# A decoder layer on one core: modulation products in groups of four, and a vector's sums inside its last step

## The chip, the core and the metric

The kernel runs on one core of a Trainium2 chip. The metric is the device time of one execution in microseconds; less is better. The engines of the core are named as in the profile: PE (the matrix engine; PEld are its weight loads), DVE (the vector engine), ACT (the scalar engine), POOL and SP. SP only issues DMA transfers here.

## The reference

One layer of a hybrid decoder for a prompt of 256 tokens and 8 sample tokens, all in float32, with a model width D of 2048 and a feed-forward width of 5632. Eleven modulation vectors (nine of the layer, two of the final norm) come from the condition c; the feed-forward blocks and the mixer use them as shift, scale and gate:

```python
mod = jax.nn.silu(c) @ p['w_ada'] + p['b_ada']
sh1, sc1, g1, sh2, sc2, g2, sh3, sc3, g3 = jnp.split(mod, N_MOD, axis=-1)
h = modulate(rmsnorm(x, p['g_ffn1']), sh1, sc1)
x = x + 0.5 * g1[:, None, :] * swiglu(h, p['w_up1'], p['w_down1'])
h = modulate(rmsnorm(x, p['g_mix']), sh2, sc2)
o, new_state = hybrid_mixer(h, lru_h0, lru_buf0, ssm_h0, ssd_buf0, p)
x = x + g2[:, None, :] * o
h = modulate(rmsnorm(x, p['g_ffn2']), sh3, sc3)
x = x + 0.5 * g3[:, None, :] * swiglu(h, p['w_up2'], p['w_down2'])
```

The matrix of one modulation vector is 2048 x 2048, 16 MB; all eleven together are 176 MB of the some 524 MB that the kernel reads.

## The kernel before, in words

The columns of the activations are the 264 tokens (COLS). Each weight is split into a high and a low part, and each product is made of three matmuls in the fp32r form: high by high, high by low, low by high (lines 1393 to 1395, in `piece`). The weights stream through the core in **steps**. A step of a feed-forward "up" or of the mixer is 8 **pieces** of 4 k-tiles by 256 weight columns, each piece 24 matmuls; a "down" step has 8 pieces of 3 or 2 k-tiles, 22 in all. For each step SP issues four weight loads (j = 0 to 3, two pieces each) into `raw` (line 489), each of which waits until DVE is done with the pieces that lay in the slot before (`lo_done`). ACT writes the high part of a piece into `w_hi` (line 608), DVE the low part into `w_lo` (line 872), and PE uses both. `w_hi` and `w_lo` have four slots, so ACT begins on piece m + 4 when PE has used piece m.

A list `plan` written out by hand sets the order: up and down steps of the first block in two chunks, then the mixer ("xbc", "dt", "lru", "z", "out"), then the second block. Each segment of the plan is a run of steps that an engine walks through either as code laid out straight or as a loop (`turns`). Segments of 4 steps per turn also carry a **modulation vector**: 16 products (`ada_product`, line 1357), four in each step, one ahead of every second piece. Two vectors are made at the start, ahead of the first step. The other nine are made inside steps: first block, chunk 0, vectors 2 and 3 in 8 up steps and vector 4 in 4 down steps; chunk 1, vectors 5 and 6 in 8 up steps and 7 in 4 down steps; second block, vector 8 in 4 up steps of chunk 0, vectors 9 and 10 in 8 up steps of chunk 1. The remaining up steps (3 or 7 of 11 in a chunk) and down steps have no products. Vectors 5 and 6, and 9 and 10, are two turns of a loop on PE; vectors 2 and 3 are laid out straight.

A product multiplies one k-tile of silu(c), `cT`, a stationary operand of 32 columns, by a slab of 128 x 2048 of the vector's matrix, in four matmuls that lie side by side in the array by `tile_position`, each with 512 columns; all sixteen add into bank b4. The slab is a load of 1 MB that SP issues (`ada_load`, line 468) into one of two slots of `ada` behind each weight load, when product a - 2 has been used. The two vectors at the start use two more slots, `ada_more`, which lie where the activations of the feed-forward blocks are later (`act_hi`).

When a vector's last step is over, its **sums** are placed: ACT copies b4 to `ada_sum` (line 621, `ada_copy`), PE transposes four blocks (line 1337, `ada_turn`), and DVE adds the bias and writes `mods` (line 894, `mod_place`). The first product of the next vector waits for that (`mod_ready`), since it writes b4. Before the change these three are the last thing that each engine does in the turn. Gates are taken from `mods` by `make_gate` into a tile of their own, and `add_branch` (line 945) adds the branch to x with it. PE starts a feed-forward block when DVE has written `h_lo` of the norm (line 923) and the first pieces.

Of the kernel before, what the change touches and what calls it, by code (L numbers as in the profile page):

```python
# [21 lines left out]
F32 = mybir.dt.float32  # L22
F32R = mybir.dt.float32r
ALU = mybir.AluOpType
# [3 lines left out]
P = 128  # L28
# [120 lines left out]
def build(nc, ins, outs):  # L149
    with ExitStack() as ctx:  # L150
# [16 lines left out]
        gate = sb("gate", [P, KD, 9])  # L167
# [21 lines left out]
        def layout(entries):  # L189
# [16 lines left out]
        _, _, ada_more, rowbuf, xrows = layout([  # L206
            ("ada_s", [P, 2, D], F32), ("ada_sum_s", [P, 512], F32), ("ada_more", [P, 2, D], F32),
            ("rowbuf", [P, ROW_TILES, P], F32), ("xrows", [P, 2, D], F32)])
        _, _, yrows, ysrow = layout([
            ("ada_e", [P, 2, D], F32), ("ada_sum_e", [P, 512], F32),  # L210
            ("yrows", [P, 2, D], F32), ("ysrow", [P, P], F32)])
# [37 lines left out]
        ada_landed = [sem(f"ada_landed{j}") for j in range(2)]  # L249
        first_landed = [sem(f"first_landed{j}") for j in range(4)]  # L250
# [205 lines left out]
        def _(sp):  # L456

            def ada_load(a, vec, k):

                if not isinstance(a, int) or a >= 2:  # L460
                    sp.wait_ge(ada_used, a - 1)
# [6 lines left out]
                sp.dma_start(ada[:, k % 2, :], src).then_inc(ada_landed[k % 2], 16)  # L468

            row_copies(sp, True, c_rows)  # L470
            for a in range(2 * KD):
                if a >= 4:
                    sp.wait_ge(ada_used, a - 3)
                dst = (ada, ada_more)[(a // 2) % 2][:, a % 2, :]
                sp.dma_start(dst, w_ada[:, a % KD, bass.ds(a // KD * D, D)]).then_inc(first_landed[a % 4], 16)
# [34 lines left out]
        def _(pool):  # L510
# [8 lines left out]
            pool.memset(outcol[:, OUT_ROWS:], 0.0)  # L519
# [3 lines left out]
            pool.wait_ge(piece_used, 8 * S_XBC)  # L523
            pool.memset(spt[:, :], 0.0)  # L524
# [73 lines left out]
        def _(act):  # L598
# [265 lines left out]
        def _(dve):  # L864
# [37 lines left out]
            def make_gate(vec, factor):  # L902
                dve.wait_ge(mod_ready, vec + 1)
                ch.link(TS(gate[:, :, :], mods[:, vec, :, :], factor, None, ALU.mult))
# [34 lines left out]
            def add_branch(s, par, before, n0, squares):  # L939
# [3 lines left out]
                for h in range(2):  # L943
                    xt = x[:, bass.ds(n0 + h, 1), 0:NT]
                    STT(xt, ps[:, h:h + 1, 0:NT], gate[:, bass.ds(n0 + h, 1), 0:1].rearrange("p a b -> p (a b)"),  # L945
                        xt, ALU.mult, ALU.add)
                xs = x[:, bass.ds(n0, 2), :]
                TT(part[:, :, NT:COLS], ps[:, :, NT:COLS], gate[:, bass.ds(n0, 2), 1:9],
# [126 lines left out]
            def dve_tasks(kind, t, j, s, o_, e_):  # L1075
# [147 lines left out]
                if kind == "z" and u == 7:  # L1223
# [22 lines left out]
                    make_gate(G2, 1.0)  # L1246
                    ch.link(dve.memset(sumsq[:, :, :], 0.0))
                if kind == "out" and j in (1, 3):
                    par = j // 2
                    add_branch(8 * (S_OUT + t) + (8 if par else 4), par, (e_, o_)[par], 2 * (2 * t + par), True)  # L1250
# [7 lines left out]
            for n, seg in enumerate(plan):  # L1258
# [14 lines left out]
                for i, last in turns(dve, seg, peel_first=n == 0, peel_last=differs(n), chain=ch, links=links):  # L1273
                    for k in range(per):
                        s, e_, o_, par = at_step(seg, i, k)
                        follows = nxt if last and k == per - 1 else PIECE_KIND[kind]
                        for j in range(4):
                            pieces_ahead(s, j, PIECE_KIND[kind], follows)
                            if kind == "up" and j == 3:
# [13 lines left out]
                            if kind == "down" and j == 3:  # L1293
                                n0 = i * (2 * per) + 2 * (what[2] + k)
                                add_branch(s * 8 + 8, par, (e_, o_)[par], n0, squares)
# [364 lines left out]
```

## Time and profile before

| What | Value |
|---|---|
| Median of 3 runs | 2333.21 us (2332.66 to 2335.88) |
| The profiled execution: its span | 2337.2 us |
| PE matmuls busy | 2185.2 us, 93% |
| DVE busy | 1200.1 us, 51% |
| ACT busy | 839.7 us, 36% |
| Read from memory | 524.37 MB, 227 GB/s over the span |
| Mean granted clock of PE | 0.967 |

The page gives no time of the profiled execution besides its span, which runs from the first to the last instruction; it is 0.17% above the median of the runs. The busy time of PE is a sum over pipelined instructions and says little by itself; the timeline shows where matmuls don't follow each other. The granted clock is 1.00 at the upper of its two levels and 0.50 at the lower one.

### The profile page before, as it was taken

Reading aid. Unit: us, or ns where it says so; the run is one execution under the profiler, and the core shown is the slowest. Engines: PE = TensorE matmul, PEld = TensorE weight load, DVE = VectorE, ACT = ScalarE, POOL = GpSimd, SP = SyncE. Lnnn points to the kernel's source line nnn. Section 1 sums busy time; section 2 is a strip of 40 time slices with the busy share of each in tenths; the row PEclk is TensorE's granted clock in tenths of the full one; section 3 lists DMA queues with packets and bytes.
Section 4 is the critical chain, followed back from the end, with each engine's and each line's share of the span. In section 5 each row is a group of like instructions: output and inputs, shape, how many; then the busy total and the mean of one; then the engine's idle time right before and its main releaser. Section 6 shows DMA issues by size and latency. Waiting matters only on the chain.

```text
span 2337.2 us, 40988 instructions
## 1 busy us (share of the span) xinstructions
PE 2185.2 (93%) x17053; PEld 1974.6 (84%) x17053; DVE 1200.1 (51%) x1602; ACT 839.7 (36%) x1020; POOL 128.9 (6%) x146
## 2 busy tenths in 40 slices
PE   4589999999999999989978889899999999999997
PEld 1178889889878898989967889789999988789996
DVE  1254345345434444576779876634445544344555
ACT  0043233334323332345544443433333433233333
POOL 0000000000000000001556200000000000000000
PEclk8799999999999999999998999999999999999998
DMA  8978895786878858746444445685545589895452
GB/s 339 365 252 297 281 305 187 256 294 225 299 262 294 280 184 298 259 138 202 158 136 135 143 158 197 220 308 194 179 153 176 187 292 302 261 307 191 149 184 86
DMA packets 380728, 533.59 MB, mean 228 GB/s; under 512 B 11815, under 2 KB 356783, under 8 KB 357807
## 3 DMA queue, kind: packets, MB, share of 16 engines
q1 hardware_dynamic: 358288, 519.28, 66.2%
q10 hardware_dynamic: 22303, 12.33, 1.8%
q8 instruction: 105, 1.72, 0.3%
q14 instruction: 32, 0.26, 0.0%
HBM read 524.37 MB, written 7.19 MB: 227 GB/s over the span
## 4 chain that ended last, share of the span: by engine, by line
PE 84%; DVE 9%; DMA 3%; ACT 2%; issue 1%; ACTq 1%; DVEq 0%; SPq 0%
PE main L1393 26%; PE main L1394 25%; PE main L1395 25%; PE b L1357 7%; DVE w_lo L872 2%; DMA ada_more<-in_w_ada 1%; DMA heads_row<-in_ssd_D 1%; DVE rec L1194 1%; ACTq L445 0%; PE b L1337 0%; ACT w_hi L608 0%; DVE cfull L1001 0%; DMA rowbuf<-in_b_ada 0%; DMA raw<-in_w_in 0%; DVE xdec L1038 0%
## 5 line engine op out<-in xcount | busy, mean ns | idle before, releaser
L872 DVE TENSOR_TENSOR w_lo<-raw,w_hi 128x1024 fp32r<-128x1024 f32 (+2 forms) x720 | 796.0, 1113 | 948.2 <-ACT w_hi L608 942.2
L1393 PE MATMUL main<-h_hi,w_hi 128*128 128x264 f32 x3664 | 1074.6, 293 | 43.3 <-DVE w_lo L872 25.7
L608 ACT ACTIVATE w_hi<-raw 128x1024 fp32r<-128x1024 f32 (+2 forms) x720 | 684.0, 956 | 1119.2 <-PE main L1395 1029.0
L1394 PE MATMUL main<-h_lo,w_hi 128*128 128x264 f32 x3664 | 1054.1, 288 | 0.0
L1395 PE MATMUL main<-h_hi,w_lo 128*128 128x264 f32 x3664 | 1052.1, 287 | 0.0
L1393 PEld LDWEIGHTS main<-h_hi,w_hi 128*128 128x128 f32 x3664 | 703.6, 192 | 146.7 <-issue 114.2
L1394 PEld LDWEIGHTS main<-h_lo,w_hi 128*128 128x128 f32 x3664 | 702.3, 192 | 2.7 <-issue 2.2
L1395 PEld LDWEIGHTS main<-h_hi,w_lo 128*128 128x128 f32 x3664 | 701.1, 191 | 0.0
L1393 PE MATMUL main<-act_hi,w_hi 128*128 128x264 f32 x1408 | 403.9, 287 | 0.0
L1395 PE MATMUL main<-act_hi,w_lo 128*128 128x264 f32 x1408 | 400.2, 284 | 0.0
L1394 PE MATMUL main<-act_lo,w_hi 128*128 128x264 f32 x1408 | 399.8, 284 | 0.0
L1393 PEld LDWEIGHTS main<-act_hi,w_hi 128*128 128x128 f32 x1408 | 264.7, 188 | 26.8 <-issue 14.3
L1394 PEld LDWEIGHTS main<-act_lo,w_hi 128*128 128x128 f32 x1408 | 265.4, 189 | 0.0
L1395 PEld LDWEIGHTS main<-act_hi,w_lo 128*128 128x128 f32 x1408 | 264.7, 188 | 0.0
L1357 PE MATMUL b<-ada,cT 128*32 128x512 f32 x1280 | 180.7, 634 | 34.6 <-DMA ada<-in_w_ada 13.8
L1357 PEld LDWEIGHTS b<-ada,cT 128*32 128x32 f32 x1280 | 26.1, 110 | 68.5 <-DMA ada<-in_w_ada 24.8
L524 POOL MEMSET spt<- 128x56 f32 x1 | 0.1, 145 | 1025.9 <-PE main L1395 1025.9
L836 ACT ACTIVATE silu_g<-main 128x528 f32<-128x528 f32 x44 | 26.9, 612 | 82.5 <-PE main L1395 82.5
L1286 DVE TENSOR_TENSOR part<-silu_g,main 128x528 f32<-128x528 f32 x44 | 31.0, 705 | 32.5 <-PE main L1395 32.5
L945 DVE SCALAR_TENSOR_TENSOR x<-main,gate,x 128x256 f32<-128x256 f32 (+1 forms) x80 | 35.0, 477 | 14.3 <-PE main L1395 14.2
L621 ACT ACTIVATE ada_sum<-b 128x512 f32<-128x512 f32 x11 | 6.4, 583 | 96.4 <-PE b L1357 96.4
L1291 DVE TENSOR_TENSOR act_lo<-part,act_hi 128x528 f32 (+1 forms) x44 | 31.2, 709 | 4.0
(219 smaller groups left out, 777.9 us busy)
## 6 DMA issues: line engine op xcount, KB each, us to landing
raw<-in_w_up SPq DMA_DIRECT2D x176, 1024.0 KB, 7.4
ada<-in_w_ada SPq DMA_DIRECT2D x128, 1024.0 KB, 5.0
raw<-in_w_down SPq DMA_DIRECT2D x96, 768.0 KB, 4.9
raw<-in_w_in SPq DMA_DIRECT2D x36, 1024.0 KB, 5.3
ada<-in_w_ada_f SPq DMA_DIRECT2D x32, 1024.0 KB, 5.4
ada_more<-in_w_ada SPq DMA_DIRECT2D x16, 1024.0 KB, 9.0
raw<-in_w_down SPq DMA_DIRECT2D x32, 512.0 KB, 3.6
raw<-in_w_out SPq DMA_DIRECT2D x16, 1024.0 KB, 5.4
```

Of the source, the lines that this page charges most:

```text
L608: A(split_view(w_hi, m, kind), raw_piece(m, kind), ACT.Copy).then_inc(hi_done, 1)
L621: A(ada_sum[:, :], b4[:, :], ACT.Copy).then_inc(ada_copied, 1)
L836: A(silu_g[:, :, :], main[:, 0:2, 0:COLS], ACT.Silu).then_inc(drained[0], 1)
L872: TT(split_view(w_lo, m, kind), raw_piece(m, kind), split_view(w_hi, m, kind).bitcast(F32), ALU.subtract).then_inc(lo_done, 1)
L945: STT(xt, ps[:, h:h + 1, 0:NT], gate[:, bass.ds(n0 + h, 1), 0:1].rearrange("p a b -> p (a b)"), xt, ALU.mult, ALU.add)
L1194: ch.link(dve.reciprocal(rec[:, :, :], rec[:, :, :]))
L1286: TT(part[:, :, :], silu_g[:, :, :], main[:, 2:4, 0:COLS], ALU.mult).then_inc(drained[1], 1)
L1291: TT(act_lo[:, bass.ds(pair * 2, 2), :], part[:, :, :], hi.bitcast(F32), ALU.subtract).then_inc(act_ready, 1)
L1357: last = MM(b4[32 * j:32 * j + 32, :], cT[:, k, :], src[:, k % 2, j * 512:(j + 1) * 512], start=k == 0, stop=k == KD - 1, tile_position=(0 ...
L1393: MM(out, wh, hi[:, k, :], start=k == 0, stop=False)
L1394: MM(out, wh, lo[:, k, :], start=False, stop=False)
L1395: last = MM(out, wl, hi[:, k, :], start=False, stop=k == total - 1)
```

## The change

All four products of a step run at its beginning, ahead of its first piece, and `ada` gets four slots; SP issues the four loads of a step together, behind the third weight load of that step, and each waits for product a - 4 instead of a - 2. `ada_more` and its semaphores go, and the two vectors at the start use the same four slots. The sums of a vector are placed inside its last step: ACT copies after its pieces of j = 1, PE transposes after the pieces of j = 2, DVE writes `mods` after its pieces of j = 3. `ada_sum` now lies in `outcol`, so POOL clears the rest of `outcol` later; gates are scaled in place in `mods`, and the separate tile goes. In the second block SP also waits for the stores of the mixer's outputs, since the larger `ada` reaches over the tile that they are read from.

```diff
-        ada, ada_sum, act_hi, act_lo = layout([
-            ("ada", [P, 2, D], F32), ("ada_sum", [P, 512], F32),
-            ("act_hi", [P, KC, COLS], F32R), ("act_lo", [P, KC, COLS], F32R)])
...
+        ada, act_hi, act_lo = layout([
+            ("ada", [P, 4, D], F32), ("act_hi", [P, KC, COLS], F32R), ("act_lo", [P, KC, COLS], F32R)])
+        ada_sum = outcol[:, 0:512]
...
             def ada_load(a, vec, k):
-                if not isinstance(a, int) or a >= 2:
-                    sp.wait_ge(ada_used, a - 1)
+                if not isinstance(a, int) or a >= 4:
+                    sp.wait_ge(ada_used, a - 3)
...
-                sp.dma_start(ada[:, k % 2, :], src).then_inc(ada_landed[k % 2], 16)
+                sp.dma_start(ada[:, k % 4, :], src).then_inc(ada_landed[k % 4], 16)
...
                             sp.dma_start(dst, unit_source(seg, i, k, j)).then_inc(w_landed[j], 16)
-                            if vec0 is not None:
+                            if vec0 is not None and j == 2:
                                 vec = i + vec0
-                                if j == 0 and k == 0 and what[0] == 1 and what[2] == 0:
+                                if k == 0 and what[0] == 1 and what[2] == 0:
                                     sp.wait_ge(h_ready, 3 * KD)
-                                ada_load(vec * KD + 4 * k + j, vec, 4 * k + j)
+                                    sp.wait_ge(stored, 16 * (len(OUT_COPIES) + 1))
+                                for q in range(4):
+                                    ada_load(vec * KD + 4 * k + q, vec, 4 * k + q)
...
@@ the pieces of ACT
+                            if vec0 is not None and k == per - 1 and j == 1:
+                                ada_copy(i + vec0)
...
-                    if vec0 is not None:
-                        ada_copy(i + vec0)
@@ the pieces of DVE
                             pieces_ahead(s, j, PIECE_KIND[kind], follows)
+                            if vec0 is not None and k == per - 1 and j == 3:
+                                mod_place(i + vec0)
...
-                    if vec0 is not None:
-                        mod_place(i + vec0)
...
-                    make_gate(G2, 1.0)
+                    dve.wait_ge(mod_ready, G2 + 1)
@@ the steps of PE
                         for j in range(4):
-                            if vec0 is not None:
-                                ada_product(i + vec0, 4 * k + j)
+                            if vec0 is not None and j == 0:
+                                for q in range(4):
+                                    ada_product(i + vec0, 4 * k + q)
...
+                            if vec0 is not None and k == per - 1 and j == 2:
+                                ada_turn(i + vec0)
...
-                    if vec0 is not None:
-                        ada_turn(i + vec0)
```

## Rows read from the trace of the kernel before

**Rows 1.** The page's chain of work that ended last, its shares by engine.
```profile
PE 84%; DVE 9%; DMA 3%; ACT 2%; issue 1%; ACTq 1%; DVEq 0%; SPq 0%
```

**Rows 2.** Stretches: us, busy time (instructions) by engine, clock, DMA share, GB/s.
```profile
core 0: us, PE busy (x) PEld busy (x) DVE busy (x) ACT busy (x) POOL busy (x), PEclk, DMA share, GB/s
58.00:59.80 1.80, 1.80 (x20) 0.30 (x12) 1.73 (x3) 0.00 (x0) 0.00 (x0) 1.00 0.99 414
...
80.00:90.00 10.00, 6.63 (x32) 0.76 (x32) 0.00 (x0) 0.00 (x0) 0.00 (x0) 0.58 1.01 424
...
240.00:244.00 4.00, 3.08 (x17) 2.27 (x18) 1.90 (x6) 0.00 (x0) 0.00 (x0) 0.75 0.31 55
...
356.00:426.00 70.00, 70.00 (x574) 70.00 (x573) 34.15 (x37) 26.18 (x27) 0.00 (x0) 1.00 0.51 169
...
447.00:468.00 21.00, 21.00 (x167) 17.08 (x166) 8.09 (x12) 6.11 (x8) 0.00 (x0) 1.00 0.99 339
```

**Rows 3.** Timeline of PE around one product: start us, us, engine, line, operation.
```profile
182.02 0.28 PE L1395 MATMUL main<-h_hi,w_lo 128*128 128x264 f32 x1
...
183.45 0.28 PE L1394 MATMUL main<-h_lo,w_hi 128*128 128x264 f32 x1
```

**Rows 4.** Timeline of PE's weight loads, products in a row before the steps.
```profile
58.37 0.12 PEld L1357 LDWEIGHTS b<-ada_more,cT 128*32 128x32 f32 x4 [0.31 <-issue]
58.80 0.12 PEld L1357 LDWEIGHTS b<-ada_more,cT 128*32 128x32 f32 x4 [0.31 <-issue]
```

**Rows 5.** Timeline of PE at the start of each feed-forward block.
```profile
118.92 0.59 PE L1393 MATMUL main<-h_hi,w_hi 128*128 128x264 f32 x1 [6.75 <-DVE w_lo L872]
...
1466.57 1.06 PE L1357 MATMUL b<-ada,cT 128*32 128x512 f32 x8
1472.28 0.56 PE L1393 MATMUL main<-h_hi,w_hi 128*128 128x264 f32 x1 [4.64 <-DVE h_lo L923]
```

**Rows 6.** Timeline of PE between vectors 2 and 3, laid out straight.
```profile
238.24 0.60 PE L1337 MATMUL b<-ident,ada_sum 128*128 128x128 f32 x4
...
240.92 0.64 PE L1357 MATMUL b<-ada,cT 128*32 128x512 f32 x4 [2.08 <-DVE mods L894]
...
249.55 0.64 PE L1357 MATMUL b<-ada,cT 128*32 128x512 f32 x4
```

**Rows 7.** Timeline at the two loop turns, between vectors 5, 6 and 9, 10.
```profile
689.75 0.49 DVE L894 TENSOR_TENSOR mods<-b,small 128x36 f32 x4
...
691.47 1.05 PE L1357 MATMUL b<-ada,cT 128*32 128x512 f32 x5 [3.46 <-issue]
...
1995.40 0.49 DVE L894 TENSOR_TENSOR mods<-b,small 128x36 f32 x4
...
1997.84 1.08 PE L1357 MATMUL b<-ada,cT 128*32 128x512 f32 x4 [4.28 <-issue]
```

**Rows 8.** DMA queues in the stretch 687 to 700: packets, MB, share.
```profile
q8 instruction: 3, 0.05, 1.9%
```

**Rows 9.** The page's costliest groups, ACT's copy of a vector's sums.
```profile
L621 ACT ACTIVATE ada_sum<-b 128x512 f32<-128x512 f32 x11 | 6.4, 583 | 96.4 <-PE b L1357 96.4
```

**Rows 10.** Timeline of ACT, DVE and SP in an up and a down step.
```profile
362.18 1.06 ACT L608 ACTIVATE w_hi<-raw 128x1024 fp32r<-128x1024 f32 x1 [1.89 <-PE main L1395]
...
364.66 0.37 SPq L489 DMA_DIRECT2D raw<-in_w_up  x1
...
432.51 0.84 ACT L608 ACTIVATE w_hi<-raw 128x768 fp32r<-128x768 f32 x1 [1.36 <-PE main L1395]
433.38 0.96 DVE L872 TENSOR_TENSOR w_lo<-raw,w_hi 128x768 fp32r<-128x768 f32 x1 [1.24 <-ACT w_hi L608]
```

**Rows 11.** The page's DMA issues: median us from issue to landing, down weights.
```profile
raw<-in_w_down SPq DMA_DIRECT2D x96, 768.0 KB, 4.9
```

**Rows 12.** Landing times of weight loads of up steps without products, 365 to 395.
```profile
DMA to landing us min/median/max: 4.9/5.0/5.1
```

More of the change, by code:

```diff
@@ L166, in build @@
         gain = sb("gain", [P, KD, 9])
-        gate = sb("gate", [P, KD, 9])
         ident = sb("ident", [P, P])
@@ L199, in layout @@
             return made
-        ada, ada_sum, act_hi, act_lo = layout([
-            ("ada", [P, 2, D], F32), ("ada_sum", [P, 512], F32),
-            ("act_hi", [P, KC, COLS], F32R), ("act_lo", [P, KC, COLS], F32R)])
[L206 to L211, printed above, removed]
+        ada, act_hi, act_lo = layout([
+            ("ada", [P, 4, D], F32), ("act_hi", [P, KC, COLS], F32R), ("act_lo", [P, KC, COLS], F32R)])
+        ada_sum = outcol[:, 0:512]
+        _, rowbuf, xrows = layout([
+            ("ada_s", [P, 4, D], F32), ("rowbuf", [P, ROW_TILES, P], F32), ("xrows", [P, 2, D], F32)])
+        _, yrows, ysrow = layout([
+            ("ada_e", [P, 4, D], F32), ("yrows", [P, 2, D], F32), ("ysrow", [P, P], F32)])
         (xbc, out_l, cin, cfull, cval, xdt, xdec, btok, cbm, s0, s0t, state, spread_b, spread_c,
@@ L248, in build @@
         w_landed = [sem(f"w_landed{j}") for j in range(4)]
-        ada_landed = [sem(f"ada_landed{j}") for j in range(2)]
-        first_landed = [sem(f"first_landed{j}") for j in range(4)]
+        ada_landed = [sem(f"ada_landed{j}") for j in range(4)]
         hi_done, lo_done = sem("hi_done"), sem("lo_done")
@@ L467, in ada_load @@
                     src = w_ada[:, k, bass.ds(vec * D, D)]
-                sp.dma_start(ada[:, k % 2, :], src).then_inc(ada_landed[k % 2], 16)
+                sp.dma_start(ada[:, k % 4, :], src).then_inc(ada_landed[k % 4], 16)
             row_copies(sp, True, c_rows)
             for a in range(2 * KD):
[L472 to L475, printed above, removed]
+                ada_load(a, a // KD, a % KD)
             for n, seg in enumerate(plan):
@@ L523, in _ @@
             pool.wait_ge(piece_used, 8 * S_XBC)
+            pool.memset(outcol[:, OUT_ROWS:], 0.0)
             pool.memset(spt[:, :], 0.0)
@@ L903, in make_gate @@
                 dve.wait_ge(mod_ready, vec + 1)
-                ch.link(TS(gate[:, :, :], mods[:, vec, :, :], factor, None, ALU.mult))
+                ch.link(TS(mods[:, vec, :, :], mods[:, vec, :, :], factor, None, ALU.mult))
             def norm_samples():
@@ L937, in norm, with add_branch @@
                 lo(KD - 1)
-            def add_branch(s, par, before, n0, squares):
+            def add_branch(vec, s, par, before, n0, squares):
                 dve.wait_ge(piece_used, s)
@@ L944, in add_branch @@
                     xt = x[:, bass.ds(n0 + h, 1), 0:NT]
-                    STT(xt, ps[:, h:h + 1, 0:NT], gate[:, bass.ds(n0 + h, 1), 0:1].rearrange("p a b -> p (a b)"),
+                    STT(xt, ps[:, h:h + 1, 0:NT], mods[:, vec, bass.ds(n0 + h, 1), 0:1].rearrange("p a b -> p (a b)"),
                         xt, ALU.mult, ALU.add)
                 xs = x[:, bass.ds(n0, 2), :]
-                TT(part[:, :, NT:COLS], ps[:, :, NT:COLS], gate[:, bass.ds(n0, 2), 1:9],
+                TT(part[:, :, NT:COLS], ps[:, :, NT:COLS], mods[:, vec, bass.ds(n0, 2), 1:9],
                    ALU.mult).then_inc(drained[par], 1)
@@ L1294, in _ @@
                                 n0 = i * (2 * per) + 2 * (what[2] + k)
-                                add_branch(s * 8 + 8, par, (e_, o_)[par], n0, squares)
+                                add_branch((G1, G3)[what[0]], s * 8 + 8, par, (e_, o_)[par], n0, squares)
                             if kind not in ("up", "down"):
                                 dve_tasks(kind, what or 0, j, s, o_, e_)
-                    if vec0 is not None:
-                        mod_place(i + vec0)
                 if kind == "down" and squares and (n + 1 == len(plan) or plan[n + 1][0] != "down"):
@@ L1341, in turn_part, with ada_product @@
                 return MM(out, src, ident[0:rows, 0:rows], start=True, stop=True)
-            def ada_product(vec, k, first=False):
-                if first:
-                    src = (ada, ada_more)[(k // 2) % 2]
-                    pe.wait_ge(first_landed[k % 4], 16 * (vec * 4 + k // 4 + 1))
-                else:
-                    src = ada
-                    pe.wait_ge(ada_landed[k % 2], (vec - 2) * (8 * 16) + 16 * (k // 2 + 1))
+            def ada_product(vec, k):
+                pe.wait_ge(ada_landed[k % 4], vec * (4 * 16) + 16 * (k // 4 + 1))
                 if k == 0:
@@ L1356, in ada_product @@
                 for j in range(4):
-                    last = MM(b4[32 * j:32 * j + 32, :], cT[:, k, :], src[:, k % 2, j * 512:(j + 1) * 512],
+                    last = MM(b4[32 * j:32 * j + 32, :], cT[:, k, :], ada[:, k % 4, j * 512:(j + 1) * 512],
                               start=k == 0, stop=k == KD - 1, tile_position=(0, 32 * j))
@@ L1426, in _ @@
             for k in range(KD):
-                ada_product(SH1, k, first=True)
+                ada_product(SH1, k)
                 if 2 <= k < 2 + batches - 1:
@@ L1433, in _ @@
             for k in range(KD):
-                ada_product(SC1, k, first=True)
+                ada_product(SC1, k)
             sumsq_total(1)
```

3 lines of the change are left out of this document (1 added, 2 removed).

## The prediction

> **What bounds the kernel.** I read four views, in this order. The chain of waits that ended last comes first: it is the matrix engine for 84% of the span, so a microsecond taken from PE in a feed-forward stage is a microsecond of the total [rows 1]. Next, the table of stages: a stage without modulation products keeps PE busy all of the time (574 matmuls in 70 us, 0.122 us each) at a DMA share of 0.51; in the down steps with products PE is busy all of the time too, but the DMA engines are as well, 0.99 at 339 GB/s [rows 2]. Two engines are near their limit there. Then the timeline of PE around one product, for what it costs, and around the ends of a vector, for what waits there. Last the issues of SP and the landing times, because the change bunches the loads.
>
> From these and the code, the two kinds of step: an up step has 8 pieces of 24 matmuls, 2.93 us each, 23.4 us; a down step has 22 x 2 x 3 = 132 matmuls, 16.1 us. Four products are added in each step that has any: 28 up steps (8, 8, 4, 8) and 8 down steps (4, 4).
>
> **Term 1, the grouping.** A product is four matmuls, recorded as eight instructions. Between the last matmul of a piece at 182.02 and the second of the next at 183.45 lie 1.43 us, where two ordinary spacings are 0.24: a product on its own costs PE 1.19 us [rows 3]. Back to back at full clock (1.00), the sets of four follow each other at 0.43 us, so a further product costs 0.86 [rows 2, 4]. Four in a row cost 1.19 + 3 x 0.86 = 3.77 instead of 4.76: 0.99 saved per step, **-35.6 us** over 36 steps. The other end is no saving (products in a row as dear as apart); I take rows 4, since they are the very instruction in the very order.
>
> Two steps differ, the first of each feed-forward block, where PE waits for the norm. In the second block the first product ends and PE then idles 4.64 us until DVE has written h_lo [rows 5]; the other three, 2.6 us, fit in, so 3 x 1.19 = 3.6 is saved there, 2.6 more than counted. In the first block PE idles 6.75 us before its first piece [rows 5] and again between the next ones, which already covers two products; the other two save 2.4, 1.4 more than counted. If the fourth load lands late there, its first piece starts late, but the pieces after it wait for DVE anyway. Together **-4.0**, with ends 0 and -7.
>
> **Term 2, the sums inside the last step.** Nine vectors are made inside steps, but only three are followed at once by a step with products, so only there does PE wait for mods. Where the code is laid out straight, PE waits 2.08 us for DVE's mods after the transposes; the granted clock is then 0.75 for 4 us, half of that stretch at the lower of its two levels, and the next product comes 8.63 us after the first, where 1.19 + 48 x 0.122 = 7.05 is usual: 1.58 lost to the clock [rows 2, 6]. In the new order the sums are placed before the last two pieces end, so **-3.7**. In the other two cases a loop starts again there. The waits are longer (3.46 and 4.28), but mods are written by 690.24 and 1995.89 and the first product starts 1.2 and 1.95 us after that; the releaser is "issue", and three transfers of the instruction queue fall in the 13 us around the first of these turns [rows 7, 8]. What is late there is PE's own instructions behind the jump back, and the jump stays. I take 0; the other end is both waits, -7.7.
>
> The moved copy (ACT, 0.58 us, [rows 9]) and the moved sums (DVE, 0.49 us, [rows 7]) cost nothing: both engines wait for PE between pieces, and the transposes are the same four. Without that cover they would cost 1.1 x 9 = 9.6. On DVE the sums now stand ahead of the last product of the step, which waits for PE's eighth piece, so nothing is queued behind them that is due. POOL's moved memset and the missing gate product of the mixer are a fraction of a microsecond: 0.
>
> **Term 3, the loads.** Before, SP put one 1 MB product load behind each weight load. Now it issues four in a row behind the third weight load, which waits until DVE has written piece 5 of the step before. That is after piece 1 is used, plus ACT's and DVE's pass: from ACT's start at 362.18 to SP's issue at 364.66, 2.5 us in up steps; 432.51 to 434.34 plus an issue, 2.3 us, in down steps [rows 10]. Counted from the first product of a step:
> - Down after down: products 3.8, two pieces 4.4, pass 2.3: issued at 10.5. The weight load lands 4.9 later [rows 11], at 15.4; four loads follow at 424 GB/s [rows 2], 2.47 us each: the fourth at 25.3. The next step's fourth product is due at 19.9 + 0.1 + 2.6 = 22.6. PE waits 2.7. There are six such steps, the second to fourth of each segment: +16.2.
> - First up step behind down steps without products (twice): 4.4 + 2.3 = 6.7, landed at 6.7 + 5.0 + 9.9 = 21.6 [rows 2, 12], due at 16.1 + 0.1 + 2.6 = 18.8: 2.8 each, +5.6.
> - Up after up: 3.8 + 5.9 + 2.5 = 12.2, landed at 27.1, due at 3.8 + 23.4 + 2.7 = 29.9. In time by 2.8, so no wait in the other up steps; behind an up step without products the down steps are in time as well.
> - The clock: a wait of 2.08 us cost 1.58 more [rows 6]. Here the wait comes in two parts with a product between them; I take half, 0.8 x 8 = +6.4, with ends 0 and +12.6.
>
> Together **+28.2**. The weight load queued behind the four is due two pieces into the next step and lands before that. The added wait of SP on stored, in the first step of the second block, is for stores issued three steps earlier, and what would queue behind it are that step's own five loads: 0.
>
> Against this load rate the Trainium skill can be weighed: "DMA: Bandwidth & Descriptors", Specifications, gives a limit of about 358 GB/s from HBM to a core. The trace shows 424 GB/s over 10 us of nothing but product loads [rows 2], so the measurement decides against it as a ceiling. By the rule a load would take 2.93 us, an estimate from that page of the Trainium skill, each of the eight waits would be about 1.8 us longer, and the sum would come out at -0.5.
>
> **Sum:** -35.6 - 4.0 - 3.7 + 28.2 = **-15.1 us**. The profiled execution has a span of 2337.2 us, 0.17% above the median of the runs, 2333.2; taken off the median this is **2318.1 us**. A measurement of this kernel can tell some 0.2% (4.7 us) from no change.
>
> **Rivals.**
> 1. *No load is late.* The burst is served faster than I think, or waits overlap with something. Then -43.3, 2290 us, and with the loop waits gone 2282. For it: the stretch at 424 GB/s. Against: even at that rate the fourth load of a down step is 2.7 us late. Chance 0.20.
> 2. *The queue is the bound, and the kernel gets slower.* A down step moves 2.88 + 4.19 = 7.08 MB; at the 339 GB/s of its stage that takes 20.9 us, just the length of the step before (16.1 + 4 x 1.19). If the mixed rate holds for the burst as well, a load takes 3.09 us, four 12.4, and the waits become 5.2 and 5.3 us: 6 x 5.2 + 2 x 5.3 = 41.8, and 6.4 to 12.6 for the clock. That gives 2338 to 2344 us. Its place is the fourth product of the eight steps named; it decides from about 4.6 us of wait per step (with 0.8 for the clock, 8 x 5.4 = 43.3). For it: share 0.99 in rows 2. Against: a burst of product loads alone is the case of 424, not of 339. Chance 0.15.
> 3. *A rate between the two.* Half way between 339 and 424, at 381 GB/s, a load takes 2.75 us and the waits are 3.8 and 3.9: 30.6, and 6.4 to 12.6 for the clock. That gives 2327 to 2333 us, no change that can be told. For it: the burst begins behind a weight load and ends before another. Against: in rows 2 nothing slows a run of product loads. Chance 0.10. The limit named in "DMA: Bandwidth & Descriptors" of the Trainium skill would be a little worse than this, 2332.7.
> 4. *The grouping saves nothing*, because the switch is paid between products too. Then terms 1 and 2 give -9.7, steps are 1 us longer and the waits 1 us shorter, 8 x 2.5 = 20: +10, 2344 us. Against: rows 4. Chance 0.05.
>
> **How the numbers follow.** The forecast has 0.50, with its own range from 1.5 us of wait and no loss of clock per place (-31, 2302) to 4 us and 1.4 (0, 2333). The range of 8 in 10 reaches to most of rival 1 and into rival 2: 2292 to 2338. Faster by over 0.2%: all of rival 1, nearly all of the forecast and a part of rival 3, 0.71. Within 0.2%: the end of the forecast and most of rival 3, 0.12. Slower: rivals 2 and 4, 0.17 with what lies beyond them.
>
> **What the new profile would show.** Right: 32 instructions of a group in about 3.6 us, an up step of 27.1 us; no wait on mods near 240; waits of 1 to 3 us on the ada loads in the two stages of down steps and at the first up step behind down steps, none elsewhere; the two loop turns still with waits on issue. Wrong: no wait on ada loads anywhere (rival 1), down steps over 24 us (rival 2), products of a group 1.2 us apart (rival 4). The forecast fails if the loads of up steps are late too, since there are 28 of them.

## The result and the profile after

The change was forecast to save 15 us; it costs a little instead. After it the kernel takes **2343.93 us** (median of 16 runs, 2335.11 to 2348.55) against 2335.34 of the kernel before in the same sessions (16 runs, 2332.66 to 2340.17): a ratio of **1.0031, 95% interval 1.0021 to 1.0041**. That is 8.6 us longer, more than the 0.2% that a measurement can tell, and above the upper end of the range, 2338. Line numbers of the new kernel: a product is line 1347, the three matmuls of a piece are lines 1383 to 1385, the transposes of the sums line 1332, `mods` line 889; SP issues weights at line 482 and product loads at line 464.

The page after first: its chain of waits by engine, the group of PE's products, and SP's product loads with their median us from issue to landing.

```profile
PE 76%; DVE 10%; DMA 9%; ACT 2%; issue 2%; SPq 1%; ACTq 1%; DVEq 0%
...
L1347 PE MATMUL b<-ada,cT 128*32 128x512 f32 x1408 | 193.3, 667 | 86.4 <-DMA ada<-in_w_ada 61.5
...
ada<-in_w_ada SPq DMA_DIRECT2D x144, 1024.0 KB, 10.3
```

Against [rows 1] PE has gone from 84% to 76% of the chain and DMA from 3% to 9%. PE waited 61.5 us in all for `ada`: 27.1 of them in the steps behind the first, where the kernel before waits for no product load (another 2.9 there are for the loads of the final norm's vectors, `in_w_ada_f`). The other 34 are at the start and in the first step, where the kernel before waits too, 25 us for `ada` and `ada_more`. So the matrix engine now waits for product loads in the steps. Where it does so is on its timeline (start us, us, and in brackets the idle time before the instruction and who ended it):

```profile
180.49 3.64 PE L1347 MATMUL b<-ada,cT 128*32 128x512 f32 x32
184.06 0.39 PE L1383 MATMUL main<-h_hi,w_hi 128*128 128x264 f32 x1
...
235.47 3.64 PE L1347 MATMUL b<-ada,cT 128*32 128x512 f32 x32
...
435.26 1.92 PE L1347 MATMUL b<-ada,cT 128*32 128x512 f32 x16
...
438.16 1.06 PE L1347 MATMUL b<-ada,cT 128*32 128x512 f32 x8 [0.97 <-DMA ada<-in_w_ada]
441.80 1.94 PE L1347 MATMUL b<-ada,cT 128*32 128x512 f32 x8 [2.57 <-DMA ada<-in_w_ada]
443.67 0.59 PE L1383 MATMUL main<-act_hi,w_hi 128*128 128x264 f32 x1
...
572.70 2.09 PE L1347 MATMUL b<-ada,cT 128*32 128x512 f32 x16
577.26 1.07 PE L1347 MATMUL b<-ada,cT 128*32 128x512 f32 x8 [2.47 <-DMA ada<-in_w_ada]
579.85 1.94 PE L1347 MATMUL b<-ada,cT 128*32 128x512 f32 x8 [1.52 <-DMA ada<-in_w_ada]
...
693.60 1.33 PE L1347 MATMUL b<-ada,cT 128*32 128x512 f32 x5 [4.49 <-issue]
697.91 5.17 PE L1347 MATMUL b<-ada,cT 128*32 128x512 f32 x27 [2.98 <-issue]
...
2002.51 1.08 PE L1347 MATMUL b<-ada,cT 128*32 128x512 f32 x4 [5.21 <-issue]
```

Line by line: at 180 a group of four products (32 instructions) runs without a gap, and the next piece starts 3.57 us after its first matmul. At 235, where PE waited 2.08 us for `mods` [rows 6], it waits for nothing now. At 435, the second of four down steps, the third product comes 0.97 and the fourth 2.57 us late; the fourth takes 1.94 us for eight instructions that take 1.06 at full clock. The first up step behind the down steps (572) has two such waits. At the loop turns (693, 2002) the idle time is put down to "issue" again, as in [rows 7], at the first turn twice; experiment 3 tests that it is PE's own instructions that are late.

SP's issues around the step at 435, and the DMA rate there (us, busy times, clock, DMA share, GB/s):

```profile
425.58 0.37 SPq L482 DMA_DIRECT2D raw<-in_w_down  x1
425.99 2.28 SPq L464 DMA_DIRECT2D ada<-in_w_ada  x4
429.49 0.38 SPq L482 DMA_DIRECT2D raw<-in_w_down  x1
```

```profile
core 0: us, PE busy (x) PEld busy (x) DVE busy (x) ACT busy (x) POOL busy (x), PEclk, DMA share, GB/s
430.00:440.00 10.00, 8.25 (x68) 5.70 (x66) 4.87 (x8) 3.38 (x4) 0.00 (x0) 1.00 1.00 417
438.20:441.80 3.60, 1.03 (x8) 0.12 (x8) 0.00 (x0) 0.00 (x0) 0.00 (x0) 0.98 1.02 380
441.80:445.00 3.20, 3.20 (x14) 1.53 (x15) 0.00 (x0) 0.00 (x0) 0.00 (x0) 0.50 1.10 349
```

The four loads are issued at 425.99; the wait for the last one ends at 441.80, 15.8 us later. The weight load of 429.49 is on the way with it. Over the last load's wait the granted clock is 0.98 on average; from its end to 445 it is 0.50. So the wait itself passes at the upper of the two levels, and the work behind it at the lower one.

### The profile page after: what moved, and what is told of

Same layout as the page of the kernel before. It is cut to its first block, busy times and chain, and to the rows that moved or that the text cites. A ratio compares the mean times of both kernels' runs of the same rounds, so it can differ in the third digit from the quotient of the medians.

```text
span 2339.0 us, 40971 instructions
## 1 busy us (share of the span) xinstructions
PE 2158.1 (92%) x17053; PEld 1974.4 (84%) x17053; DVE 1199.6 (51%) x1601; ACT 840.8 (36%) x1020; POOL 129.9 (6%) x146
## 4 chain that ended last, share of the span: by engine, by line
PE 76%; DVE 10%; DMA 9%; ACT 2%; issue 2%; SPq 1%; ACTq 1%; DVEq 0%
PE main L1383 23%; PE main L1384 23%; PE main L1385 23%; DMA ada<-in_w_ada 6%; PE b L1347 5%; DVE w_lo L867 3%; DMA heads_row<-in_ssd_D 1%; ACT w_hi L603 1%; SPq L464 1%; DVE rec L1189 1%; DVE ntile L923 1%; DMA ada<-in_w_ada_f 1%; ACTq L441 0%; DVE h_lo L918 0%; PE b L1332 0%
## 5 line engine op out<-in xcount | busy, mean ns | idle before, releaser
L1347 PE MATMUL b<-ada,cT 128*32 128x512 f32 x1408 | 193.3, 667 | 86.4 <-DMA ada<-in_w_ada 61.5
L1347 PEld LDWEIGHTS b<-ada,cT 128*32 128x32 f32 x1408 | 39.0, 115 | 198.9 <-DMA ada<-in_w_ada 111.2
L940 DVE SCALAR_TENSOR_TENSOR x<-main,mods,x 128x256 f32<-128x256 f32 (+1 forms) x80 | 34.8, 476 | 14.2 <-PE main L1385 14.2
L616 ACT ACTIVATE outcol<-b 128x512 f32<-128x512 f32 x11 | 6.5, 592 | 96.8 <-PE b L1347 96.8
```

Of the source, the lines that this page charges most:

```text
L940: STT(xt, ps[:, h:h + 1, 0:NT], mods[:, vec, bass.ds(n0 + h, 1), 0:1].rearrange("p a b -> p (a b)"), xt, ALU.mult, ALU.add)
L1347: last = MM(b4[32 * j:32 * j + 32, :], cT[:, k, :], ada[:, k % 4, j * 512:(j + 1) * 512], start=k == 0, stop=k == KD - 1, tile_position=(0 ...
```

## The experiments

The theory from this profile: the fourth load of a burst lands late in certain steps, and that eats what the grouping saved. The rivals: the queue is the bound whatever the order (the prediction's rival 2); the grouping or the sums save less than thought; the new cost lies at the loop turns. Each run has its own median against runs of the kernel before in the same session (medians 2334.06, 2336.12 and 2334.35); a difference to the changed kernel is one to its median of 2343.93, from other sessions. No experiment leaves computation out; one adds some. In `e2_spread` a product is line 1346.

**1. The burst two weight loads earlier** (`e1_early`): the same four slots, the same bytes, only SP's place in its queue is another.

```diff
-                            if vec0 is not None and j == 2:
+                            if vec0 is not None and j == 0:
```

> The four product loads of a step go behind its first weight load instead of its third; nothing else changes, and the same bytes move. Theory 1, the loads are issued too late: in the changed kernel PE waits for them 4.8, 3.7, 3.7 and 4.9, 3.9, 3.6 us in the down steps, 5.4 and 3.4 us at the first up step behind down steps, 1.8 and 3.0 us in the second step of each block, 38 us together, and 3 to 9 us go to the clock behind them. All of it goes: 41 to 47 us less than the changed kernel, 2297 to 2303 us. Rival, the DMA queue is at its limit in the down steps: the waits move to other loads, at most 10 us come back, 2334 us or more.

Measured: **2290.84 us**, ratio 0.9814 (0.9802 to 0.9827), 43.2 us less than before and 53.1 less than the changed kernel (50.7 by the two ratios). That is 6 us lower than the theory expected. Its timeline of PE, of SP, and the stretch of a whole down step:

```profile
434.50 3.64 PE L1347 MATMUL b<-ada,cT 128*32 128x512 f32 x32
...
671.76 1.11 PE L1347 MATMUL b<-ada,cT 128*32 128x512 f32 x5 [3.35 <-issue]
674.80 5.92 PE L1347 MATMUL b<-ada,cT 128*32 128x512 f32 x27 [1.93 <-issue]
```

```profile
415.74 2.90 SPq L464 DMA_DIRECT2D ada<-in_w_ada  x4
418.69 15.28 SPq L482 DMA_DIRECT2D raw<-in_w_down  x4
```

```profile
core 0: us, PE busy (x) PEld busy (x) DVE busy (x) ACT busy (x) POOL busy (x), PEclk, DMA share, GB/s
434.28:454.15 19.87, 19.87 (x167) 17.09 (x165) 8.19 (x13) 6.34 (x8) 0.00 (x0) 1.00 0.96 354
```

The loads of the step at 434 are issued at 415.74, 18.8 us ahead of its first product, where the changed kernel has 9.3. Behind the first step, which waits 5.0 us for product loads, no step waits for one any more: every group but those at the loop turns takes its 3.6 us, a down step 19.87 us at clock 1.00. The same 7.08 MB that rival 2 gave 20.9 us pass in that at 354 GB/s, so the queue wasn't the bound. The late burst costs the whole gain and more.

With this run as the measure, the changed kernel's steps can be set beside steps that wait for nothing. Worked out from the timelines: the length of a step is the time from the last matmul ahead of its group to the last ahead of the next group, "over" is what it has over the same step of `e1_early` (at 948 over a group's 3.78 us), "waits" the idle times put down to `ada` in it. (The waits named in the expectation above are what a group takes over 3.78 us, the lower clock included.) The last column is a second profile of the changed kernel (`e12_again`, below).

```
step (start in the profile after)       length  over  waits   over, 2nd profile
151.22  second up step, block 1          29.05  1.82   1.51   1.74
435.05  down step 2, chunk 0             25.32  5.45   3.54   5.42
460.37  down step 3                      23.60  3.73   3.10   3.82
483.97  down step 4 (and 3 without)      88.52  3.76   3.13   4.46
572.49  first up step behind down        34.21  6.99   3.99   6.49
899.04  down step 2, chunk 1             25.46  5.59   3.63   5.46
924.50  down step 3                      23.79  3.92   3.31   3.80
948.29  down step 4                             3.61   2.32   3.40
1505.68 second up step, block 2          30.23  3.01   2.60   2.80
1884.32 first up step behind down        30.57  3.35   2.93   3.07
sum                                            41.2   30.1   40.5
the two loop turns                              5.2           2.9
mixer, from 948 to 1474                         3.1           0.2
```

The other steps with products agree with `e1_early` to 0.04 us in the first profile, but for the first of each block, which waits for the norm (-1.4 and +0.3).

**2. One load behind each weight load** (`e2_spread`): four slots and groups as in the change, but the loads spread as before it.

```diff
-                            if vec0 is not None and j == 2:
+                            if vec0 is not None:
...
-                                for q in range(4):
-                                    ada_load(vec * KD + 4 * k + q, vec, 4 * k + q)
+                                ada_load(vec * KD + 4 * k + j, vec, 4 * k + j)
```

> One product load behind each weight load, as before the change, but with four slots and the grouped products. Theory 1 (issued too late): in a down step the last load goes out about 15 us after the step's first product and lands near 21, before it is due at 22.6, so as little is late as with all four behind the first weight load: 2297 to 2305 us. Rival, the queue at its limit: 2334 us or more, as in the other order.

Measured: **2320.91 us**, 0.9945 (0.9933 to 0.9957): a miss by 16 us or more. Its timelines of PE and SP at the first up step behind the down steps show why:

```profile
563.67 3.08 PE L1346 MATMUL b<-ada,cT 128*32 128x512 f32 x24
572.26 1.93 PE L1346 MATMUL b<-ada,cT 128*32 128x512 f32 x8 [5.51 <-DMA ada<-in_w_ada]
```

```profile
558.02 0.37 SPq L482 DMA_DIRECT2D raw<-in_w_up  x1
558.58 1.81 SPq L464 DMA_DIRECT2D ada<-in_w_ada  x1
```

Three products are in time, but the last load stands behind the fourth weight load and is issued only 5.1 us ahead of the group. It lands 13.6 us after its issue, 5.51 us late. A group at the beginning of a step needs all four loads then; spread, the last one comes later than in the burst (8.6 us after the start of the group, against 7.1 at the same step of the changed kernel).

**3. The loop turns** (`e3_unrolled` on the changed kernel, `e7_before_unrolled` on the one before): PE's segments with products laid out straight.

```diff
-                for i, last in turns(pe, seg, peel_first=n == 0):
+                for i, last in turns(pe, seg, peel_first=vec0 is not None):
```

> The changed kernel with PE's code for the vectors laid out straight, no loop on PE in those segments; loads and order stay. Theory, PE waits at the two loop turns for its own instructions behind the jump back: the 10.4 and 8.2 us lost there (wait, second wait, lower clock) go, 2344 - 18 = 2326 us. Rival, the wait there is for the sums or for instructions in any layout: no change, 2340 to 2347 us.

> The kernel before with PE's code of the vector segments laid out straight. Theory, the two loop turns lose 9.0 and 7.0 us there for late instructions, and without the jump what is left is the wait for the sums, 2.1 us and 1.6 us of clock each: 2334 - 16 + 7 = 2325 us. Rival, the wait there is for the sums alone: no change, 2334 us.

Measured: **2323.77 us**, 0.9951 (0.9933 to 0.9969), and **2326.45 us**, 0.9955 (0.9942 to 0.9969). Laid out straight, the changed kernel has its group at that turn without a gap, and still its late loads; the kernel before has a shorter wait there, for DVE:

```profile
441.58 1.07 PE L1347 MATMUL b<-ada,cT 128*32 128x512 f32 x8 [2.78 <-DMA ada<-in_w_ada]
...
693.43 3.64 PE L1347 MATMUL b<-ada,cT 128*32 128x512 f32 x32
```

```profile
689.35 1.77 PE L1357 MATMUL b<-ada,cT 128*32 128x512 f32 x8 [2.39 <-DVE mods L894]
...
1985.12 1.07 PE L1357 MATMUL b<-ada,cT 128*32 128x512 f32 x8 [2.48 <-DVE mods L894]
```

So at the turns the wait for the jump covers the wait for `mods`. The transfers of the instruction queue between 687 and 704 agree: four in the changed kernel, one in `e3_unrolled` (the DMA view of each, packets, MB, share):

```profile
q8 instruction: 4, 0.07, 1.6%
```

```profile
q8 instruction: 1, 0.02, 0.4%
```

**4. The sums, undone alone** (`e4_sums_late` on the changed kernel; `e6_early_sums_late` on `e1_early`; `e9_eu_sums_late` on experiment 5): `ada_copy`, `ada_turn` and `mod_place` go back behind the last step. The edit on ACT; the other two are alike:

```diff
-                            if vec0 is not None and k == per - 1 and j == 1:
-                                ada_copy(i + vec0)
...
+                    if vec0 is not None:
+                        ada_copy(i + vec0)
```

> The changed kernel with the copy, the transposes and the sums of a vector placed after its last step again; grouping and loads stay. Theory, they are worth what the straight turn between vectors 2 and 3 showed, 2.1 us of wait and 1.6 us of clock, and nothing at the loop turns, where instructions are late anyway: 2344 + 4 = 2348 us. Rival, the sums are what PE waits for at the loop turns too: 2344 + 4 + 2 x 3 = 2354 us or more. Third, the order of the sums costs what the change loses: 2335 us.

> e1 with a vector's copy, transposes and sums placed after its last step again, so that nothing but the grouping and the loads differ from the kernel before. Theory, the sums inside the last step are worth 3.7 us at the straight turn and 1 to 6 us at the two loop turns: 2295 to 2300 us. The grouping alone is then the rest, 35 to 40 us under the kernel before. Rival, the sums are worth nothing (as e4 against the changed kernel seems to say): 2291 us.

> e5 (loads behind the first weight load, no jumps in PE's vector segments) with the copy, the transposes and the sums of a vector after its last step again. Without late loads and without the jump, the sums show alone, at all three places where a step with products follows. Theory, they are worth 2.1 to 2.5 us of wait and up to 1.6 us of clock each: 2278 + 7 to 12 = 2285 to 2290 us. Rival, worth nothing: 2278 us.

Measured: 2342.59 us, 1.0042 (1.0028 to 1.0056), which can't be told from the changed kernel's 1.0031: the 4 us of the theory are too small to be seen here, the two other expectations (2354 or more, and 2335) are out; 2294.6 us, 0.9818 (0.9805 to 0.9832), not to be told from `e1_early` by the ratio; and **2284.81 us**, 0.9793 (0.978 to 0.9807), 6.5 us over its base by the medians, with the intervals of the two ratios apart. The traces are clearer. In `e4_sums_late` the wait on `mods` at 235 is back; in `e9_eu_sums_late`, which has no loop turns, there are such waits at the former turns too:

```profile
236.77 3.64 PE L1347 MATMUL b<-ada,cT 128*32 128x512 f32 x32 [2.08 <-DVE mods L889]
```

```profile
671.32 5.18 PE L1347 MATMUL b<-ada,cT 128*32 128x512 f32 x32 [2.39 <-DVE mods L889]
...
1948.92 3.64 PE L1347 MATMUL b<-ada,cT 128*32 128x512 f32 x32 [2.48 <-DVE mods L889]
```

Placing the sums inside the last step does what it says, at three places; with the loop turns left, no gain was seen at two of the three.

**5. Both repairs** (`e5_early_unrolled`): the edits of experiments 1 and 3 together.

> Loads behind the first weight load (as e1) and PE's code of the vector segments laid out straight (as e3). Theory, at the loop turns PE waits for instructions behind the jump back: in e1 they cost 8.7 and 4.7 us beyond a product group, 13.4 together, so 2291 - 13 = 2278 us. Rival, the two gains overlap, since the lower clock behind the waits was common to both: 2285 us or more.

Measured: **2278.33 us** (2275.42 to 2279.62), 0.9747 (0.9734 to 0.976). It beats both kernels: 58 us under the one before, 66 under the changed one.

**6. The group two pieces later** (`e8_late_group`): the loads stay where the change put them, PE takes its products ahead of the third piece.

```diff
-                            if vec0 is not None and j == 0:
+                            if vec0 is not None and j == 1:
```

> The changed kernel with its loads where they are, behind the third weight load, but the four products of a step two pieces later, ahead of its third piece. Theory, a load is late because it is due too soon behind its issue: the products are now due 4.4 us later in a down step and 5.9 us later in an up step, more than most of the waits (3.6 to 5.4 us), so 0 to 1 us is left at each place: 2292 to 2305 us. Rival, the waits come from the loads as a burst on the queue, whenever they are used: 2335 us or more.

Measured: **2295.03 us**, 0.9822 (0.9809 to 0.9836). At 437.68 stands a whole group of 32 instructions, and no step waits for a load. So it is the time from issue to use that decides, whichever end of it is moved.

**7. The burst one weight load later** (`e10_fourth`), the same lead made shorter:

```diff
-                            if vec0 is not None and j == 2:
+                            if vec0 is not None and j == 3:
```

> The changed kernel with the four product loads behind the fourth weight load of a step, two pieces later than the third. Theory (issue time decides): counted from the last product of a step to the next, an up step takes 1.1 + 11.7 + 2.5 to the issue and 15.7 to the last landing, 31.0 us, where 27.2 are needed, so now the up steps wait too, 3.8 us each at 24 of them; down steps 6.7 us at six, 8 us at the two first up steps, 2.4 at two: 152 us of waits instead of 38, and 1 to 1.5 us of clock at each of 34 places instead of 14 in all: 2480 to 2500 us. Rival (the queue is the bound, issue time matters little): 2344 to 2370 us.

Measured: **2517.04 us**, 1.0777 (1.076 to 1.0794), clock 0.934: right in kind, 17 us above the expectation. Now the up steps wait as well, and the third and fourth products run at half clock there:

```profile
182.73 1.06 PE L1347 MATMUL b<-ada,cT 128*32 128x512 f32 x8
185.22 1.07 PE L1347 MATMUL b<-ada,cT 128*32 128x512 f32 x8 [1.43 <-DMA ada<-in_w_ada]
187.71 1.94 PE L1347 MATMUL b<-ada,cT 128*32 128x512 f32 x8 [1.43 <-DMA ada<-in_w_ada]
190.25 1.94 PE L1347 MATMUL b<-ada,cT 128*32 128x512 f32 x8 [0.60 <-DMA ada<-in_w_ada]
```

**8. The waits filled with matmuls** (`e11_busy`): in the second to fourth down step of a segment six matmuls stand ahead of each of the third and the fourth product; their result is used by nobody. The loads are as late as before, but PE idles less.

```diff
+                                    if kind == "down" and k and q >= 2:
+                                        for _ in range(6):
+                                            MM(b7[:, 0:P], ones[:, :], ident[:, :], start=True, stop=True)
                                     ada_product(i + vec0, 4 * k + q)
```

> The changed kernel with six matmuls of two constants into an idle bank ahead of the third and of the fourth product of the second to fourth down step of both segments, where PE waits for loads otherwise; the result doesn't use them. Theory, the waits stay, but PE is busy in them and its granted clock stays at the upper level there: 5 to 9 us less than the changed kernel, 2335 to 2339 us, and the clock is 1.00 right behind those six places. Rival, the clock is not part of the loss: 2344 us or more, since a matmul that is still running when the load lands only delays the product.

Measured: **2326.13 us**, 0.9962 (0.9949 to 0.9976): 17.8 us less than the changed kernel, more than expected. The stretch of the down steps, first of `e11_busy`, then of the changed kernel (columns as above):

```profile
430.00:495.00 65.00, 64.28 (x519) 53.38 (x519) 22.87 (x34) 17.12 (x22) 0.00 (x0) 1.00 0.83 308
```

```profile
430.00:495.00 65.00, 55.24 (x432) 43.60 (x431) 21.29 (x33) 16.90 (x21) 0.00 (x0) 0.97 0.84 313
```

With the waits filled the clock stays at 1.00. But in its trace the steps at 435, 460, 484, 899 and 924 are only 3.9 us shorter together; the fourth step of chunk 1 and the mixer behind it are 4.9 shorter and the loop turns 5.2, though the filler isn't at the turns or in the mixer. So the clock behind a wait is a cost of its own, some 4 us in these five steps. The mixer and the turns are also where two profiles of the unaltered kernel differ (experiment 9, 2.9 and 2.3 us), so what is gained there can't be put down to the filler.

**9. The changed kernel once more** (`e12_again`), no edit, for a second profile.

> The changed kernel, unaltered, for a second profile. The first profiled execution took 2340.7 us, 3.3 below the median of the 16 runs (2343.9), at a mean clock of 0.966 where the longest run, 2348.55, had 0.959. Step lengths in the first profile: the ten steps with a late load are 41.2 us longer together than the same steps of the kernel with the loads behind the first weight load, the two loop turns 5.2 us longer, the mixer 3.3. Theory A, the clock behind late loads varies from execution to execution: if this one is longer than 2340.7, at least two thirds of the difference stand in the ten steps (more than 41.2) and at the loop turns, with more stretches at half clock behind the late loads, and the waits on the loads themselves stay at 30 us within 1. Theory B, the difference is anywhere (start, mixer, norms): the ten steps stay at 41 within 1.5 us and the rest grows.

Measured: 2334.16 us (one run; the kernel before took 2334.03 beside it), shorter than the first profiled run, so theory A's condition isn't met as it was put. Of the 6.5 us between the two spans 0.8 lie in the ten steps (40.5 us over against 41.2, last column of the table) and 2.3 at the loop turns, less than theory A's two thirds; 2.9 lie in the mixer and 0.8 at the start. For these two executions theory B fits.

Two other traces speak for theory A. `e3_unrolled` and `e4_sums_late` have the same loads in the same places. Their waits for them in the ten steps are 30.8 and 29.7 us, against 30.1 and 29.4 in the two profiles above, but the steps are 49.0 and 43.2 us over. The difference is the clock: the lower level follows the late loads at the places of 460 and 484 in both and in `e3_unrolled` at those of 1505 and 1884 too, while in `e4_sums_late` it stays away at those of 899 and 948. The fourth product of the step at 460, in the changed kernel and then in `e3_unrolled`, behind waits of the same length:

```profile
466.87 1.06 PE L1347 MATMUL b<-ada,cT 128*32 128x512 f32 x8 [1.45 <-DMA ada<-in_w_ada]
```

```profile
467.48 1.94 PE L1347 MATMUL b<-ada,cT 128*32 128x512 f32 x8 [1.48 <-DMA ada<-in_w_ada]
```

So the waits are steady, and the clock behind them isn't: the late loads cost 40.5 to 49.0 us in four executions.

## Why the prediction was wrong

**The reading of the kernel held.** Groups of 3.57 us where 3.77 was forecast less a spacing; an up step of 27.23 us (27.1 forecast), a down step in time 19.88 (19.9). With no load late the kernel takes 43.2 us less than before, where rival 1 had 43.3 (2290 us; 2290.84 measured). That is closer than its parts, and some of it luck. Between the profiles of the kernel before and of `e1_early`, 47.0 us apart, 30 plain steps save 27.8 us where 0.99 each makes 29.7, the first steps of the two blocks 7.0 (6.0 forecast with their grouping), the straight turn 4.7 (as forecast), and 5.6 us lie at the loop turns and in the mixer, where nothing was forecast. Term 1 and Term 2 were right within some 2 us. The wait on `mods` at 240 is gone, the loop turns stay, and straight code takes their wait away: what is late there is PE's instructions behind the jump. The Trainium skill ("Runtime: NRT & Kernel Launch", Instruction fetch mechanics) says that a taken jump to a page outside the current window must wait for a DMA fetch of that page; the four instruction transfers against one agree with it.

**The step that failed is Term 3: its size.** Eight of its ten places were right, its issue times nearly so (425.9 forecast for the step at 435, 425.99 seen), its sum was not: +28.2 forecast, 41.2 in the profile.
- *Landing.* Four loads at 2.47 us behind a weight load of 4.9 make 14.8 us; the last is there after 15.8. The rate was right: 417 GB/s from 430 to 440. (The Trainium skill, "DMA: Bandwidth & Descriptors", Specifications, gives a limit of about 358 GB/s from HBM to a core; this trace, with its 417, is above it.) What the term left out is the instruction queue, one of whose transfers falls into the time of this burst (the DMA view of 425.90 to 441.80):

```profile
q8 instruction: 1, 0.02, 0.4%
```

  The burst of 939.23, with the next weight load 3.5 us behind it as well, has none (the view of 939.20 to 953.80 has no line of that queue), and its last load is there after 14.6 us. The times from issue to landing of the four loads, of 425.99 and then of 939.23:

```profile
DMA to landing us min/median/max: 7.2/10.1/13.9
...
DMA to landing us min/median/max: 7.0/9.9/12.7
```

  The share of 0.4% of 16 engines in 15.9 us is 1.0 us of one engine's time. Of the 35 bursts for the steps behind the first, 24 have a transfer of that queue end between the landing of the weight load ahead of them and that of their last load; these take 11.1 to 11.6 us from the one to the other, and the 11 without it 10.0 to 10.5. No run moved these transfers, so the cause is read from this split alone. The waits in the six down places are 2.3 to 3.6 us, not 2.7, and in the two first up steps 3.99 and 2.93, not 2.8: 26.0 against 21.8.
- *What a late load costs besides.* 0.8 us per place was taken for the clock. Besides the marked waits the eight steps are 10.5 us longer (36.4 less 26.0), not 6.4: 1.3 to 3.0 us each where half clock followed (435, 572, 899, 948), 0.4 to 0.6 at 460, 484, 924 and 1884, where it did not, but products came one at a time.
- *Two places not foreseen*, the second step of each feed-forward block: 4.8 us. The step ahead begins behind the norm, the burst is issued at 139.58 for a first product at 151.43, 11.9 us ahead, and its last load lands 16.2 us after the issue; the second place has 10.4 us. The forecast had up steps in time by 2.8 us and used the pass of an undisturbed step for all of them; in undisturbed up steps no load was late.

Term 3 at 41.2 alone would have given some 2331 us, inside the range. Term 3 and the loop turns of the first profile (18.6 us over two plain steps, against 16.0 before) turn -15.1 into about +0.5, and the spans of the profiled executions differ by +1.8 (2339.0 and 2337.2). **The rest stays open.** The profiled execution of before was long for its kernel (2337.2 and some 1.7 us around the span, against a median of 2335.3), that of after short (2340.68 against 2343.93): 6.8 us, of no known place. The times of the changed kernel go with the mean clock (2335.11 us at 0.966, 2348.55 at 0.959), and they spread over 13.4 us where the five runs of `e1_early` lie within 4. The ten steps alone took 7.8 us more in the profile of `e3_unrolled` than in the first of the changed kernel, 7.1 of them besides the waits (experiment 9), and the eight runs of `e3_unrolled` spread over 20 us. So the clock behind late loads can be much of the rest; no run near the median was profiled, so it was not shown.

**The rivals.** Rival 2 gave nearly the right time (2338 to 2344) for a wrong reason: the queue as the bound is refuted by experiments 1 and 6, which move the same bytes without these waits, though its sign, a down step over 24 us, shows in two of six (25.3 and 25.5). Rival 3's slower rate isn't there, since four loads take 10.0 to 10.5 us where no transfer of the instruction queue falls in; with one they take 11.1 to 11.6, as much as its 11.0, so it had the landing nearly right for another reason. The waits, 3.2 us on average in the down places and 3.5 in the up places, lie between the forecast's and its own. Rival 4 is refuted by the groups. The forecast's own range, with 4 us of wait and 1.4 of the clock at eight places, reached 43.2 us, so it had room for Term 3 at 41.2, though not for ten places; it had none for longer loop turns and for the part that stays open.

## What to carry to other kernels

More slots give a load room, not time: what counts is the time from its issue to its use, the place in the issuing queue sets that, and with bursts the last load decides, together with what else the DMA engines carry meanwhile (here some 1.2 us with a transfer of the instruction queue). So put a burst at the earliest point at which its slots are free, and work out the lead for the steps that are disturbed (behind a norm, behind shorter steps) as well as for the plain ones. A late load on a busy matrix engine costs more than its wait; count the broken-up group and the clock besides, and the clock as a range, since the same wait was followed by the lower level in one execution and not in another.

## What the runs showed of the hardware

The jump at a loop turn of four steps costs more than the wait in front of the first product: in the changed kernel 4.49 us, then 2.98 more five instructions later, the step being 10.4 us over a plain one, and 8.2 at the second turn. Laying PE's code straight took 20 us off the changed kernel (2343.9 to 2323.8) and 12.5 off `e1_early`. And with twelve idle-time matmuls in each of six steps, whose result nobody uses, the kernel took 17.8 us less by the medians; 3.9 us of that are seen in five of these steps, and the part outside the down steps was not expected and is not explained.
